# Group B's logits are placed between the products of the pair before, a fourth hosted tile goes to ScalarE, and the edges of the stages are rewritten

## The reference

```python
h -> rmsnorm -> one projection -> heads of group A and of group B
# group A: 8 heads x 64, one shared key and value; an index score chooses 256 keys for each query
score = sum_h relu(qi_h . ki) * wi_h ; sel = top_k(score, 256)
p = softmax(qa . ka / 8 - slope * |distance|)  over sel ; out = p @ va
# group B: 4 heads, two maps each, values of 128, chunk-causal
p = softmax(qb . kb / 8 - slope * |distance|)  for both maps
out = (p[0] - lam * p[1]) @ vb ; rmsnorm over the head
o = concat(A, B) ; h = h + o @ w_o ; h = h + relu(rmsnorm(h) @ w_up)**2 @ w_down ; y = rmsnorm(h)
```

## Time and profile before

| | us |
|---|---|
| median of 3 runs | 3878.54 (3877.07 to 3885.38) |
| profiled execution | 3880.51, its span 3878.7 |
| `project_keys`, `project_queries` | 0 to 301, 301 to 641 |
| `attend_sample` | 641 to 977.6 |
| `attend_prompt` tiles 0 to 7 | 977.6 to 1324.9 |
| `feed_forward` | 1324.9 to 2197.6 |
| `attend_prompt` tiles 8 to 15 | 2197.6 to 2926.2 |
| `feed_forward` | 2926.2 to 3878.7 |
| PE busy | 3504.6 (90% of the span) |
| DVE, ACT, POOL busy | 2142.1, 1867.5, 254.8 |

### The profile page before, as it was taken

How to read it: one execution, slowest core, us unless ns; L and a number is a source line. 1 busy time by engine, 2 the same in 40 slices (tenths; PEclk the granted TensorE clock), 3 DMA queues, 4 the chain that set the end, 5 groups by cost and what they waited for, 6 DMA issues and landing times. The chain is left out here.

```text
span 3878.7 us, 49946 instructions
## 1 busy us (share of the span) xinstructions
PE 3504.6 (90%) x19049; PEld 2953.6 (76%) x19049; DVE 2142.1 (55%) x3853; ACT 1867.5 (48%) x2907; POOL 254.8 (7%) x442
## 2 busy tenths in 40 slices
PE   8998997776799689998999699999996999999997
PEld 6886786334588578887888488888885888799996
DVE  4334764887466367777776555555553434443333
ACT  2213443664366367786776255565552333332331
POOL 1000010000010110002000100001001000100000
PEclk9998998887799899999999799999998999999998
DMA  5547445541831322433432441111104323322221
GB/s 156 156 139 233 148 151 186 191 154 25 209 77 43 132 87 87 143 116 120 143 108 96 142 140 36 48 38 42 35 6 142 109 98 109 131 81 72 87 70 45
DMA packets 231295, 419.86 MB, mean 108 GB/s; under 512 B 28832, under 2 KB 129184, under 8 KB 221856
## 3 DMA queue, kind: packets, MB, share of 16 engines
q1 hardware_dynamic: 189808, 333.93, 26.8%
q0 software_dynamic: 17072, 71.68, 5.6%
q10 hardware_dynamic: 24192, 11.24, 1.1%
HBM read 336.69 MB, written 80.12 MB: 107 GB/s over the span
## 5 line engine op out<-in xcount | busy, mean ns | idle before, releaser
L1293 PE MATMUL rPV<-rV,rPTr 128*128 128x64 f32 (+1 forms) x2592 | 337.6, 271 | 0.7 <-ACT rPTr L1361 0.7
L1293 PEld LDWEIGHTS rPV<-rV,rPTr 128*128 128x128 f32 x2592 | 326.2, 191 | 10.8 <-issue 1.1
L2478 ACT ACTIVATE gRU<-gUP 128x512 f32<-128x512 f32 (+1 forms) x64 | 41.8, 653 | 497.7 <-PE gUP L2318 497.7
L1361 ACT ACTIVATE rPTr<-rTP 128x512 f32<-128x512 f32 (+1 forms) x360 | 189.2, 553 | 164.2 <-PE rTP L1282 161.6
L1345 ACT ACTIVATE rX<-rX,rmx 128x1168 f32<-128x1168 f32 (+7 forms) x128 | 210.7, 1646 | 116.2 <-DVE rmx L1423 115.9
L2318 PE MATMUL gUP<-gA_hi,gW_hi 128*128 128x320 f32 (+2 forms) x784 | 222.9, 334 | 7.8 <-DVE gW_lo L2520 6.1
L2318 PE MATMUL gUP<-gA_hi,gW_lo 128*128 128x320 f32 (+2 forms) x784 | 222.6, 334 | 0.0
L2318 PE MATMUL gUP<-gA_lo,gW_hi 128*128 128x320 f32 (+2 forms) x784 | 222.5, 334 | 0.0
L2318 PE MATMUL fUP<-fA_hi,fW_hi 128*128 128x512 f32 (+1 forms) x544 | 208.0, 382 | 15.2 <-DVE fW_lo L2520 11.2
L951 ACT ACTIVATE fajunk<-faS,fav 128x2064 int8<-128x2064 f32 (+4 forms) x120 | 205.6, 1714 | 12.1 <-DMA y<-fY 9.8
L2520 DVE TENSOR_TENSOR fW_lo<-fW_raw,fW_hi 128x2048 fp32r<-128x2048 f32 x72 | 163.4, 2291 | 81.4 <-ACT fW_hi L2420 81.4
(11 more groups left out here) (408 smaller groups left out, 8761.2 us busy)
## 6 DMA issues: line engine op xcount, KB each, us to landing
fW_raw<-w_up SPq DMA_DIRECT2D x32, 1024.0 KB, 5.1
fW_raw<-w_down SPq DMA_DIRECT2D x32, 1024.0 KB, 5.0
gW_raw<-w_up SPq DMA_DIRECT2D x32, 1024.0 KB, 5.0
gW_raw<-w_down SPq DMA_DIRECT2D x32, 1024.0 KB, 4.9
qT<-qOUT SPq DMA_DIRECT2D x40, 512.0 KB, 3.3
sKB<-cache_kb SPq DMA_DIRECT2D x8, 2048.0 KB, 13.5
sVB<-cache_vb SPq DMA_DIRECT2D x8, 2048.0 KB, 8.1
kT<-ktz ACTq DMA_DIRECT2D x17, 640.0 KB, 4.1
```

The source lines that it names most:

```text
L1293: mm = pe.matmul(pv[:, 0:size], PTr[n % 3][:, j - 4 * k, :], V[:, j, a:a + size], start=(j == 0), stop=(j == blk[t] - 1))
L1361: act.activation(PTr[n % 3][:, 0:size, :], TP[bank_use[("p", n)] % 2][:, 0:size, :], ACT.Copy).then_inc(s_pt, 1)
L2478: act.activation(RU[:, 0:nt * P].rearrange("p (n w) -> p n w", n=n), UP[f % 2][:, 0:n, 0:width], ACT.Relu).then_inc(s_ru, 1)
```

## The change

Eight edits, by stage:
- `project_queries`: in the last group the units are spread over one step less.
- `attend_prompt`: the first block of queries, the first keys and the nearest part of the distances are loaded first; the lambda arithmetic stands behind the first two takes; the logits of odd jobs of group B leave the even job's slot and stand, piece by piece, between the products of the applied job (g + 2 and g + 3 there).
- `attend_sample`: ACT's list gets tile 4 (DVE's loses it), `PLAN` is new, the own selection is spread over six jobs in place of seven, new keys come by DMA on SP's queue in place of POOL's copy.
- `feed_forward`: the first two `TR` loads are issued by ACT and their parts stand ahead of the first weights'; SP issues the stores of `y` in the last group.

```diff
+        steps = QBLK - 1 if gi < NGR - 1 else QBLK - 2
+        return mine[len(mine) * max(bi - 1, 0) // steps:len(mine) * min(bi, steps) // steps]
...
-                early = g + AHEAD < NG and groups[t] > 1
+                G = groups[t]
+                ahead = [j for j in ((g + AHEAD,) if m < H_A else (g + AHEAD - 1, g + AHEAD)) if j < NG]
+                units = [(j, k) for j in ahead for k in range(halves[j // JOBS])]
+                def logits_between(i):
+                    for u, (j, k) in enumerate(units):
+                        at = u if m > H_A else 0 if u == 0 and G > 1 else G - 1
+                        if i == min(at, G - 1):
+                            logits(j, slice(k, k + 1))
                 transposes(0)
-                for k in range(1, groups[t]):
+                for k in range(1, G):
                     transposes(k)
-                    if k == 1 and early:
-                        logits(g + AHEAD, slice(0, 1))
+                    logits_between(k - 1)
                     products(k - 1)
-                if g + AHEAD < NG:
-                    logits(g + AHEAD, slice(1, None) if early else slice(None))
-                products(groups[t] - 1)
+                logits_between(G - 1)
+                products(G - 1)
...
                 if applied(g):
                     apply(g)
-                elif g + AHEAD < NG:
-                    logits(g + AHEAD)
...
+            softmax(0)
+            softmax(1)
             act.wait_ge(s_lam, 2)
             act.activation(lv[:, 2:4], lv[:, 0:2], ACT.Exp).then_inc(s_lam, 1)
-            softmax(0)
-            softmax(1)
...
-    PLAN = [(0, 0)] * 2 + [(2, 5)] * (B - 2) + [(1, 3), (6, 4)] * B + [(2, 7)] * B
+    PLAN = [(0, 0)] * 2 + [(2, 4)] * (B - 2) + [(1, 2), (5, 2)] * (B - 2) + [(1, 5), (5, 6)] * 2 + [(7, 6)] * B
...
+            def new_keys(b):
+                sp.dma_start(KB[b % 2][:, :, PAST:SKEYS], KN[:, 1:5, b * Q:(b + 1) * Q]).then_inc(s_kb[b % 2], 16)
...
-                pool.tensor_copy(KB[b % 2][:, :, PAST:SKEYS], KN[:, 1:5, b * Q:(b + 1) * Q]).then_inc(s_kb2, 1)
...
-            SPAN = B - 1
+            SPAN = B - 2
...
+                    for t in range(nt):
+                        sp.wait_ge(s_t5, g * NT1 + t + 1)
+                        sp.dma_start(y[token(g, t):token(g, t) + P, :], Y[:, t, :]).then_inc(s_ye, 16)
+                    sp.wait_ge(s_ye, 16 * nt)
...
-EARLY = [7, 6, 5], [4, 3, 2, 1]
+EARLY = [7, 6, 5, 4], [3, 2, 1]
```

More of the change, by code:

```diff
@@ L1084, in attend_prompt @@
         s_d0 = sem("s_d0")
+        s_q0 = sem("s_q0")
+        s_first = sem("s_first")
         s_x0 = sem("s_x0")
@@ L1164, in store @@
                 sp.dma_start(oT[:, :, (T0 + t) * P:(T0 + t + 1) * P], OT[:, :, :]).then_inc(s_fs, 16)
-            queries(QA, 0, 0, H_A, s_qa)
-            keys(0)
-            for dst, src in ((DT[:, :], dist), (idn[:, :], ident), (lam4, lambdas), (gB[:, :], sub_g)):
+            first, rest = (slice(0, 1), slice(1, ABLK))
+            for part, done in ((first, s_q0), (rest, s_qa[0])):
+                for copy in range(2):
+                    sp.dma_start(QA[0][copy * DH:(copy + 1) * DH, :, :, :].bitcast(F32)
+                                 .rearrange("d (h b) u q -> d h b (u q)", h=2)[:, :, part, :],
+                                 qT[T0, :, part, :, :].rearrange("(h d) b u q -> d h b (u q)", h=2)).then_inc(done, 16)
+                if part == first:
+                    keys(0)
+                    sp.dma_start(DT[:, nearest[0]:PKEYS], dist[:, nearest[0]:PKEYS]).then_inc(s_d0, 16)
+            for dst, src in ((idn[:, :], ident), (DT[:, 0:nearest[0]], dist[:, 0:nearest[0]]), (lam4, lambdas),
+                             (gB[:, :], sub_g)):
                 sp.dma_start(dst, src).then_inc(s_c, 16)
@@ L1388, in _ @@
                 dve.memset(X[i][:, :], 0.0).then_inc(s_x0, 1)
[L1390 to L1400, removed]
             dve.wait_ge(s_x0, XB)
@@ L1484, in _ @@
                 dve.scalar_tensor_tensor(DA[0][:, 0:n_of[0]], DA[0][:, 0:n_of[0]], -BIG,
-                                         DT[:, nearest[0]:PKEYS], ALU.mult, ALU.add).then_inc(s_d0, 1)
-                dve.wait_ge(s_d0, 1)
+                                         DT[:, nearest[0]:PKEYS], ALU.mult, ALU.add).then_inc(s_first, 1)
+                dve.wait_ge(s_first, 1)
             take(0)
             take(1)
+            dve.wait_ge(s_c, 64)
+            for i in range(2):
+                dve.tensor_tensor_reduce(out=OM[:, i * DH:(i + 1) * DH], in0=lam4[:, 2 * i, :],
+                                         in1=lam4[:, 2 * i + 1, :], scale=1.0, scalar=0.0,
+                                         op0=ALU.mult, op1=ALU.add, accum_out=lv[:, i:i + 1]).then_inc(s_lam, 1)
+            dve.wait_ge(s_lam, 3)
+            dve.tensor_tensor(lv[:, 4:5], lv[:, 3:4], lv[:, 2:3], ALU.subtract).then_inc(s_lam, 1)
+            dve.wait_ge(s_lam, 4)
+            dve.tensor_scalar(lv[:, 5:6], lv[:, 4:5], -LAM_INIT, None, ALU.add).then_inc(s_lam, 1)
+            dve.tensor_scalar(gB[:, :], gB[:, :], 1.0 - LAM_INIT, None, ALU.mult).then_inc(s_lam, 1)
+            dve.wait_ge(s_lam, 6)
             for g in range(NG):
@@ L2110, in feed_forward @@
         s_o = [sem(f"s_o{i}") for i in range(2)]
+        s_o0 = [sem(f"s_o0{i}") for i in range(2)]
         s_ohi = sem("s_ohi")
```

49 lines of the change are left out of this document (29 added, 20 removed).

## The result

The changed kernel takes 4021.2 us (4020.2 to 4022.8); the kernel before took 3880.7 beside it. The ratio is 1.0362 (1.0344 to 1.0380). The forecast was 3964.5, within 3910 to 3990: the side was right, the size wrong, 140 us in place of 86.

What follows compares the result with a forecast made beforehand. It took the bound in `attend_prompt` to be the loop of DVE's combine and takes and ACT's exponentials; 79 + 34 - 4 - 6.5 - 6 - 8 - 2.3 = +86 on 3880.5, less 2.0, gave 3964.5 us, range 3910 to 3990.

Steps and rivals of the forecast that it cites:

- +79: `attend_prompt`, tiles 8 to 15: spreading the odd job's logits lengthens 31 intervals between combines, +79 us, bounds 43 and 105.
- +34: `attend_prompt`, tiles 0 to 7: one more logits job and products(0) enter the loop, +34 us, bounds 17 and 40.
- the price on ACT in `attend_sample`: `attend_sample`: 45 halvings left to ACT behind the ninth job's exponential take 108.3 us against 74.9, so +33.4.
- the wait for POOL: `attend_sample`: PE's wait for POOL's copy of new keys, 16.0 us, goes, as a transfer replaces the copy.
- the heads of `feed_forward`: Start of both `feed_forward` stages: loads move the same bytes over the same engines at the same time, so nothing.
- The loop's sum: `attend_prompt`, tile 12: parts from one combine's end to the next add to 12.03 us against 9.18, +2.85 a pair.
- The ends: End of both `feed_forward` stages: with SP storing, POOL's powers run ahead, -6.5 us and -6, bounds 1.8 and 9 each.
- The head of the second prompt stage: Start of the second `attend_prompt`: the first take no longer waits behind lambda and the mask, -8 us, bounds -4 and -9.5.
- The first, that the spread pays: Rival on `attend_prompt`: transposes run while DVE takes, so PE's idle time at pair heads goes; 3818 us, chance 0.09.
- New keys late (the third): Rival on `attend_sample`: the new keys' transfer has short runs and lands late, stage ends 20 us later; 3988, chance 0.11.
- Half the price (the second): Rival on `attend_prompt`: the second piece waits for the copy in some tiles only, 43 and 17; 3911 us, chance 0.12.
- hidden halvings (the fourth): Rival on `attend_sample`: ACT's halvings are hidden and the stage gains 25 us and more; about 3940, chance 0.06.

Runs made afterwards that it cites:

- e5: The changed kernel with the first piece of the odd job's logits computed three times, as more work on PE: 4014.5 us, ratio 1.0343.
- e1: The changed kernel with group B's logits back in their old places, all else of the change kept: 3882.8 us, ratio 0.9996.
- e6: e1 with group A's values loaded behind the last stream's loads in `attend_sample`, not behind the fourth's: 3872.5 us, ratio 0.9972.
- e8: e1 with the lists, plan and span of the hosted selections as before the change: 3870.9 us, ratio 0.9960.
- e7: e1 with the first two loads of attention output in `feed_forward` back on POOL, behind the first weights: 3872.6 us, ratio 0.9970.
- e2: The kernel before with the spread of the logits alone: 4032.2 us, ratio 1.0369.
- e3: The changed kernel with all pieces of the odd job's logits ahead of products(0), behind the first transposes: 3912.3 us, ratio 1.0068.
- e11: e1 with e6's values order, e8's old plan and lists, six-job span, and `feed_forward` rows loaded first on SP's queue: 3858.5 us, ratio 0.9933.

## Where the prediction was right, and which of its steps failed

The change is 54 us more than forecast. The step that failed first is the price of the loop, the terms +79 and +34: its path through the engines was right, but its parts were priced at the durations of full clock, and the loops took +97.1 and +43.3 (the second without 6.4 that isn't the loop's). Beside it, the price on ACT in `attend_sample` was 10.5 too low, the wait for POOL there went only in part, and the heads of `feed_forward`, put at nothing, cost 6 to 7 each.

**The odd job's logits, tiles 8 to 15: mechanism right, size too small, by the clock.** The loop's sum was 12.03 for tile 12; at full clock 12.14 was measured. The estimates at the ends, +1.4 and +3.4, were +1.3 (9.00 against 7.67) and +2.8 (15.02 against 12.20). The term of the sum that was mis-sized is the +79, which measured +97.1. Its parts were priced at the durations of the earlier trace rows, which PE shows at full clock. In tile 12 the change makes PE wait 2.25 us in each pair, and behind this wait PE works for a time at 1.2 GHz in two pairs of three. Within tiles, 24 intervals grew by 75.4 us. At each tile's lowest interval they would have grown by 60 (61 by the sum); for tile 13, of whose three intervals none stands at full clock, this takes the 12.83 of e5. Fourteen of the 24 have a granted clock of 0.99 or 1.00; the other ten, at 0.82 to 0.90, make up the difference. e5 shows that the irregular part vanishes in tiles 10 to 14 when the wait is filled. The seven intervals from one tile to the next grew by 21.7, the sum had 18.

**The same, tiles 0 to 7: the same step, and an interval that isn't the loop's.** +34 was +49.7 between the stage's combines. Within tiles 24 intervals grew by 33.3, and at each tile's lowest interval they would have grown by 25 (26 by the sum). Tile 5's pair is 5.9 at full clock (6.08 by the sum) and 7.6 at a mean of 0.78. No filler was tried in tiles 0 to 6, since what is issued ahead of that wait is in the loop, so that the clock makes the whole of the difference is argued from the windows and not shown. The seven intervals from one tile to the next grew by 16.4 (8 by the sum), and 6.4 of it stands between tile 0 and tile 1, where the sum has 0.25. This interval scatters without the spread too: in the seven runs with the logits in their old places it takes 19.6 to 25.1, and e1's +4.5 is there. The longer it is, the lower is its granted clock. The changed kernel and, in a fence of its own, e6:

```profile
1023.10:1049.80 26.70, 24.52 (x104) 0.50 0.98 257
```

```profile
1016.50:1036.10 19.60, 14.31 (x107) 1.00 1.09 285
```

What sets the clock there from run to run is open.

**`attend_sample`: two terms of it.** Ahead of the ninth job 37.6 were forecast; 35.2 came (240.0 from the stage's start to the exponential before, 204.8 after). The term "the wait for POOL, 16.0, goes" was mis-sized: 9.7 of the 16.0 stood at the fifth job, whose keys had landed only 2.5 us before PE went on. The row names POOL as the last to come, but most of that wait was the load's, behind the sixteen loads of values. It stayed, as 8.6. e6 took it away. The other is the price on ACT, 33.4, which was 43.9. Some 4 us of the difference lie in the five jobs with seven halvings: one takes 16.92 and not 16.13, as the products between the copies ran at half clock (eight of them 1.94 us in place of 1.08; the mean clock is 0.67 over these jobs), and ACT's last copy waits 1.85 behind them in place of 0.88. The other 5.7 stand at the tenth job, whose exponential waits for DVE's take behind two closings; the sum had no such wait. e8 shows that this price is the larger one.

**The edges.** The ends came as forecast or better: from the last product to the next stage, 7.2 less in f and 9.1 in g. The step that failed is "its loads at the head move the same bytes over the same engines at the same time: nothing". PE's first product came 9 to 10 us later, since ACT now waits for the rows and they land later, and 6 to 7 of that stayed; e7 gets back 4.5 in f and 6.5 in g. The head of the second prompt stage, up to its first combine, was 65.0 before; in the eleven kernels with the new head it is 56.4 to 63.0, so it gave 2 to 8.6, where 8 were forecast. The short ones stand at a clock of 0.86 or 0.87, the long ones at 0.78 to 0.82.

**The rivals.** The first, that the spread pays, is refuted by e1 and e2. Its condition, that the second take's last piece starts no later than 4.0 us behind the first take, fails in the changed kernel (7.66 in tile 12). In e3 it is met (3.99), and the spread costs next to nothing there, but it gains nothing either: the loop through DVE and ACT is as long as before, whether PE waits in it or not. So the rule of the Trainium skill's page Perfetto Trace Analysis, section Optimization Strategy, that the prediction cites, to find the gaps of the most contended engine and start sooner what they wait for, didn't lead to a gain here: PE's waits for the take, 34.4 us in the earlier trace rows, are 4.9 now, but 95.6 of waits for ACT's copy have come. New keys late (the third) came true once, at another place and by another cause than that rival named. Half the price (the second) and hidden halvings (the fourth) are refuted: both terms came out above the forecast.

## What to carry to other kernels

Before work is moved on one engine into a gap, follow the loop through the other engines' fixed orders: a piece that lands behind a result which another engine makes late takes that whole detour into the loop. Price a loop that gets new waits on PE at both clocks. And where a wait for an engine's copy ends just behind a landing, it is the load that is to be moved, not the copy.

## What the runs showed of the hardware

**PE's clock falls inside a pair.** With one wait of 2.0 to 2.3 us in each pair, windows stand at 0.87 (tile 12) and 0.78 (tile 5); with the wait cut to 0.42 the clock stays at 1.00. In the changed kernel's tiles 8 and 9, where the waits are 1.3 to 1.5, all six intervals stand at 1.00, in tile 13, where they are 2.49, all three stand at 0.88, and in tile 15, with up to 2.96, one of three stands at 0.99. In the kernel before, tile 12's pairs have a wait of 0.82 to 0.88 and stand at 1.00:

```profile
2589.22 1.97 PE L1261 MATMUL rLG<-rK,rQB 128*128 128x512 f32 x8 [0.88 <-DVE rmx L1423]
```

```profile
2588.00:2597.20 9.20, 8.32 (x61) 1.00 0.01 2
```

The Trainium skill's page TensorE: Matmul & The Clock Gate, section HAM oscillation, tells of a kernel whose clock falls at each wait for data, so that every round starts cold. The trace agrees, but not in each round: of tile 12's three intervals two are slow and one isn't, though its wait is as long (2.26). In e2, which has the same code there, it is the second that is fast (12.13 beside 12.86 and 13.76). Why a given one is fast stays open.

**Loads that are issued together land far apart.** The DMA issues at the head of g (KB each, median us from issue to landing), after:

```profile
gW_raw<-w_o SPq DMA_DIRECT2D x2, 1024.0 KB, 9.6
...
gTR<-oT ACTq DMA_DIRECT2D x2, 512.0 KB, 17.2
```

On ACT's queue 512 KB of rows take 17.2 us beside SP's and POOL's loads; before, on POOL's queue behind the first weights, the first two landed 8.5 and 10.1 us after their issue. The Trainium skill's page DMA: Bandwidth & Descriptors, section Queues, rings and completion order, says that a DMA engine takes turns between its queues packet by packet. If the profile's packets are meant, that would leave a queue of short packets the smaller share, and the trace agrees in direction: 1.05 MB in 2080 packets on ACT's queue, 2.10 MB in 1056 on SP's, in the first 20 us. No run here changes the packets alone, so this cause isn't shown. The first place on SP's queue doesn't help either: in e11 the weights stand behind the rows and land 13.0 and 16.1 us after their issue, where the changed kernel has 5.5 and 5.6.
